# A hybrid stream encoder on one core: sums of squares and turned roots of a recurrence as 64x64 products, with new tables for the order of all its items

## The chip, the cores and the metric

The kernel runs on one NeuronCore of one Trainium2 chip. A core has a matrix engine (TensorE, PE in the profile; its weight loads are shown as an engine of their own, PEld), a vector engine (DVE), a scalar engine (ACT), a GpSimd engine (POOL) and a queue for transfers (SyncE, SP). The metric is the device time of one execution in microseconds (us), as the median of several runs; lower is better.

## The reference

The reference is one inference step of a small encoder in float32: a layer with an RWKV-7 time mixer and a layer with banded attention, each followed by a gated feed-forward part. The change touches the time mixer alone:

```python
kk = heads(k * k_k)
kk = kk / jnp.maximum(jnp.sqrt(jnp.sum(kk * kk, axis=-1, keepdims=True)), 1e-12)
...
def step(S, inp):
    r_t, w_t, k_t, v_t, na_t, b_t = inp
    sa = jnp.einsum('bhvk,bhk->bhv', S, na_t)
    S = S * w_t[:, :, None, :] + sa[..., None] * b_t[:, :, None, :] + v_t[..., None] * k_t[:, :, None, :]
    return S, jnp.einsum('bhvk,bhk->bhv', S, r_t)
...
mean = jnp.mean(out, axis=-1, keepdims=True)
var = jnp.mean(jnp.square(out - mean), axis=-1, keepdims=True)
out = ((out - mean) * lax.rsqrt(var + LNX_EPS)).reshape(B, T, D) * lnx_w + lnx_b
```

There are 16 heads of 64 channels, 1024 prompt frames, and 8 streams of 16 frames: 1152 frames in all. Two sums over the 64 channels of a head are needed for each frame: one of the squared keys (`kk * kk`) and one of the squared, centered outputs (`var`).

## The kernel before

The recurrence (`recurrence_phase`) works on pairs of heads: one pair fills the 128 partitions, head one in partitions 0 to 63 and head two in 64 to 127, with the 1152 frames as columns. There are 8 pairs. The frames are cut into 18 chunks of 64 and, for wide work, into three thirds of 384 columns. Everything is written as a list of items, `(what, pair, argument)`. All engines walk through one list, `ITEMS_ORDER`, in order (TensorE through `TENSOR_ORDER`, the same list with some items joined), and each does its own part of an item; semaphores carry the dependences. So the order of the list is the order of every engine's queue.

The list is made of six threads, each with a letter. A is the serial part (`step`, two parts for each of 16 chunks, and the eight streams' steps `s0t`, `sw`, `so`, `ns`, `nst`). B forms the matrices of a chunk (`form`). C prepares a pair (`w`, `a`, `scan`, `ksum`, `decays`, `kexp`, `k2`, `b`, `write`, `rk`). D finishes a pair (`center`, `vsum`, `affine`, `gate`). E and F invert the chunks' triangular matrices in groups of four chunks, on two lines (`x0`, then `invert` with a half 0 and a half 1 for each level, then `fold`). A string of letters, `PATTERN`, says from which thread the next item comes. It is used for every pair, with the serial part of pair o, the finishing of pair o-1 and most of the forming and inverting of pair o+1. Another string, `FIRST`, comes ahead of it once, and has no A in it.

Three facts of the code matter here.

- `heads` issues two 64x64 products that stay in their head's half (partitions 0 to 63 to 0 to 63, and 64 to 127 likewise). `cross` issues two that change the half. The profile shows a float32 product of these as two matmuls and two weight loads.
- `joined` merges neighbours of the list on TensorE: an `invert` half 1 beside a `form` becomes `both`, a `step` part 0 with an `invert` half 0 right behind it becomes `beside`. In these the products of the two alternate.
- `sums` (L1350) takes the sums of squares as nine 128x128 products with 56 columns of `headones`; `expanded` (L1357) turns the roots of a third back into rows of channels by three 128x128 transposes. `ksum` and `vsum` are one item for a pair each, `kexp` and `affine` three each. Their results go to one PSUM bank, bank 7 (`PIECE_BANKS`), which they share with `w`, `a`, `rk`, `center`, `gate` and others; a piece has to be read before the next is written.

What stands behind a sum: DVE scales the sums (L1779 or L1813) and inverts them (L1781, L1815), ACT takes the root of all 1152 columns (L1697, L1700) after a table load, TensorE turns it (`kexp`, `affine`), DVE multiplies.

Of the kernel before, what the change touches and what calls it, by code (L numbers as in the profile page):

```python
# [373 lines left out]
def front_phase(nc, t, mem, o):  # L374
# [468 lines left out]
SUM_COLS = 56  # L843
# [7 lines left out]
FIRST = (  # L851
    "CCCCCCCCCCCCCCCCCCCCBBBCCCBCCCCBCCEBECBBEBCBCECFFBCFCCFCCFEBFCFCEBCCFCCCBEBEBFCECCFECFECCCE")
PATTERN = (
    "EBADFBAEDABEAFDFEADAFBAEFAAECDADADBFECAFEACFBEBCFAEDAECCAABFAEADAECAFCEADABFCEABECACFAEACEAAEFCAFCAEECABABFAAA"
    "EFACBEACAFBECCAACFACEBBFCAAEAFCEBBECAAEFCEAFEACFCCE")
# [138 lines left out]
def prepare_items(o):  # L994
# [4 lines left out]
    out += [("ksum", o, None)] + [("decays", o, c) for c in range(3)]  # L999
# [4 lines left out]
def finish_items(o):  # L1004
    return [("center", o, c) for c in range(3)] + [("vsum", o, None)] + [("affine", o, c) for c in range(3)] + [("gate", o, c) for c in range(3)]


def last_finish_items():
    o = PAIRS - 1
    center, vsum, rest = (lambda x: (x[:3], x[3], x[4:]))(finish_items(o))  # L1010
    return center + [("ns", o, 1), vsum] + rest[:3] + [("nst", o, 0), ("nst", o, 1)] + rest[3:]
# [18 lines left out]
def recurrence_order():  # L1030
# [30 lines left out]
    for c, after in enumerate((("vsum", o, None), ("affine", o, 2), ("nst", o, 0))):  # L1061
        for_tensor.remove(("gate", o, c))
        for_tensor.insert(for_tensor.index(after) + 1, ("gate", o, c))
# [11 lines left out]
    ("high", 1, "vsum", None), ("high", 5, "vsum", None), ("high", 6, "nst", 0))]  # L1075
PIECE_BANKS = (7, 0, 1, 2, 3, 4)
LAST_BANKS = {("center", 0): 4, ("center", 1): 5, ("ns", 1): 4, ("nst", 0): 5, ("affine", 1): 5, ("affine", 2): 4,
# [4 lines left out]
def recurrence_phase(nc, t, mem, o):  # L1082

    m = recurrence_areas(mem)
    with ExitStack() as ctx:
# [27 lines left out]

        head_sums = lambda pb: pb[:, 0:T // P * SUM_COLS].rearrange("p (i h c) -> p i h c", h=2, c=SUM_COLS // 2)[:, :, :, 0]
        roots = lambda j: m.rs[:, j, :].rearrange("p (i h) -> p i h", h=2)
# [219 lines left out]
        def _(pe):  # L1335
# [53 lines left out]
            def read(pr, n):  # L1389

                pe.wait_ge(outs_done, NCH * pr + n + 1)
                cross(out_of(n), m.s[:, n % 2, :], m.ar[:, pr % 2, n, 64:128], False, False).then_inc(read_done, 1)

# [60 lines left out]
            STREAMED = {("w", 0): 30, ("w", 1): 4, ("w", 2): 4, ("a", 0): 4, ("a", 1): 4, ("a", 2): 4, ("ksum", None): 4,  # L1454
                        ("kexp", 0): 12, ("kexp", 1): 5, ("kexp", 2): 5, ("rk", 0): 28, ("rk", 1): 4, ("rk", 2): 4}
            STREAMED_LAST = {("center", 0): 3, ("ns", 1): 4, ("vsum", None): 4}
            for key in TENSOR_ORDER:
# [6 lines left out]
                if what in PIECES:  # L1464
# [10 lines left out]
                elif what == "ksum":  # L1475
                    pe.wait_ge(kq_ready, pr + 1)
                    sums(pb, m.k2).then_inc(piece_done[b], 1)
                elif what == "kexp":
                    pe.wait_ge(kroot, pr + 1)
# [2349 lines left out]
```

## Time and profile before

| what | us |
|---|---|
| median of 3 runs | 3540.37 (3538.47 to 3543.31) |
| the profiled execution's own time | 3546.33 |
| its span in the profile | 3544.6 |
| TensorE busy (share of the span) | 3381.6 (95%) |
| DVE, ACT, POOL busy | 1652.6, 1354.5, 1740.5 |
| the recurrence in the span | about 412 to 1130 |
| first `step` of pairs 0 to 7 at | 493.9, 570.1, 652.1, 733.1, 812.2, 896.7, 978.6, 1053.9 |

The span is the time from the first to the last instruction. A "busy" engine has at least one instruction under way; matmuls overlap, so a busy TensorE can still go faster. "Idle" is shown with what ended it; "issue" is idle time in which the engine waited for nothing that the profile shows. The granted clock is TensorE's share of its full clock.

### The profile page before, as it was taken

To read this page: it belongs to the slowest core of one execution; us is meant where nothing else is said; L and a number is where in the kernel's file an instruction comes from. 1 tells how busy PE (TensorE), PEld (TensorE's weight loads), DVE (VectorE), ACT (ScalarE), POOL (GpSimd) and SP (SyncE) were. 2 spreads that over 40 slices of the span, in tenths; PEclk is the share of its full clock that TensorE was granted. 3 is DMA by queue.
4 is the path that set the end of the run, shared out by engine and by line. 5 is a ranking of instruction groups with operands and counts; after the bars stand their busy time and mean duration, and the time that the engine had idled before them with its cause. 6 is when DMAs were issued, how large, how long until landed. Compare 5 with 4: busy or idle time off the path is not lost. (4 is left out here: it accounts for less than half of the span.)

```text
span 3544.6 us, 87445 instructions
## 1 busy us (share of the span) xinstructions
PE 3381.6 (95%) x33525; PEld 2940.6 (83%) x33525; DVE 1652.6 (47%) x3032; ACT 1354.5 (38%) x2917; POOL 1740.5 (49%) x1622
## 2 busy tenths in 40 slices
PE   8999889998898999999999999999989999999999
PEld 8999778777777998888888887777769988888887
DVE  7113356555554374444444533333343744444444
ACT  6212445554443133333333434444453333333335
POOL 4434266666654445454554544344433354545455
PEclk9999899999999999999999999999999999999999
DMA  4422211111114011111111234444442111111111
GB/s 154 154 88 89 71 35 36 43 41 38 38 44 143 10 45 46 48 44 45 44 46 47 87 85 96 114 102 91 107 108 66 41 46 47 43 50 42 47 44 73
DMA packets 432743, 233.86 MB, mean 66 GB/s; under 512 B 190979, under 2 KB 417043, under 8 KB 431558
## 3 DMA queue, kind: packets, MB, share of 16 engines
q1 hardware_dynamic: 428882, 215.40, 21.9%
q10 hardware_dynamic: 3572, 14.33, 1.0%
q8 instruction: 215, 3.52, 0.4%
q14 instruction: 74, 0.61, 0.1%
HBM read 187.69 MB, written 47.21 MB: 66 GB/s over the span
## 5 line engine op out<-in xcount | busy, mean ns | idle before, releaser
L2688 DVE TENSOR_TENSOR H<-ps,H 128x512 f32<-128x512 f32 x608 | 419.6, 690 | 463.3 <-PE ps L2351 462.5
L2239 POOL TENSOR_TENSOR split<-work,split 128x512 fp32r<-128x512 f32 x280 | 379.8, 1361 | 493.9 <-ACT split L2510 486.8
L2351 PE MATMUL ps<-split,split 128*128 128x512 f32 x1824 | 514.0, 390 | 0.0
L2404 PE MATMUL ps<-xs,split 128*128 128x512 f32 x1920 | 512.5, 393 | 0.0
L1341 PE MATMUL ps<-arena 64*64 64x64 f32 (+1 forms) x9984 | 400.9, 225 | 37.9 <-issue 21.2
L1341 PEld LDWEIGHTS ps<-arena 64*64 64x64 f32 x9984 | 351.6, 135 | 71.4 <-issue 45.6
L2404 PEld LDWEIGHTS ps<-xs,split 128*128 128x128 f32 x1920 | 349.9, 188 | 68.2
L2351 PEld LDWEIGHTS ps<-split,split 128*128 128x128 f32 x1824 | 339.8, 188 | 70.9 <-DVE H L2688 0.7
L2404 PE MATMUL ps<-split,split 128*128 128x512 f32 x1440 | 366.1, 390 | 0.5 <-issue 0.5
L3278 PE MATMUL ps<-xs,split 128*128 128x384 f32 x1656 | 361.4, 355 | 2.6 <-POOL split L3192 2.6
L601 PE MATMUL ps<-mixed,wsplit_mix 128*128 128x384 f32 x1872 | 331.7, 339 | 7.6 <-DVE mixed L824 7.6
L601 PEld LDWEIGHTS ps<-mixed,wsplit_mix 128*128 128x128 f32 x1872 | 330.1, 189 | 8.9 <-DVE mixed L824 8.9
L1347 PE MATMUL ps<-arena 64*64 64x64 f32 (+3 forms) x4448 | 305.6, 253 | 27.9 <-DVE arena L1853 9.6
L2404 PEld LDWEIGHTS ps<-split,split 128*128 128x128 f32 x1440 | 267.6, 188 | 55.5 <-issue 1.0
L3278 PEld LDWEIGHTS ps<-xs,split 128*128 128x128 f32 x1656 | 277.9, 189 | 30.0 <-issue 22.4
L1347 PEld LDWEIGHTS ps<-arena 64*64 64x64 f32 x4448 | 209.4, 136 | 62.8 <-issue 43.5
L2510 ACT CAST split<-work 128x512 fp32r<-128x512 f32 x280 | 174.0, 622 | 138.8 <-PE ps L2404 107.7
L2244 POOL TENSOR_TENSOR split<-work,split 128x256 fp32r<-128x256 f32 x168 | 132.6, 790 | 173.1 <-ACT split L2517 170.5
L3441 ACT ACTIVATE work<-work,work 128x640 f32<-128x640 f32 (+3 forms) x144 | 101.0, 702 | 257.4 <-DVE work L3532 249.4
L3244 POOL TENSOR_SCALAR work<-work,work 128x640 f32<-128x640 f32 (+2 forms) x64 | 95.0, 1484 | 190.0 <-DVE work L3537 190.0
L95 POOL TENSOR_SCALAR wsplit_mix<-stage_mix 128x1024 fp32r<-128x1024 f32 x26 | 76.1, 2927 | 203.7 <-PE ps L601 171.4
L2548 ACT COPY ps<-ps 128x512 f32<-128x512 f32 x120 | 68.8, 573 | 279.1 <-PE ps L2404 279.1
(325 smaller groups left out, 5972.4 us busy)
## 6 DMA issues: line engine op xcount, KB each, us to landing
work<-in_ffn_w_gu SPq DMA_DIRECT2D x168, 256.0 KB, 2.9
work<-in_ffn_w_down SPq DMA_DIRECT2D x168, 128.0 KB, 2.3
work<-in_cache_v SPq DMA_DIRECT2D x64, 256.0 KB, 3.9
work<-in_cache_k SPq DMA_DIRECT2D x256, 64.0 KB, 2.2
rkv_scratch<-lora ACTq DMA_DIRECT2D x24, 576.0 KB, 2.8
stage_mix<-in_rwkv_w_rkv SPq DMA_DIRECT2D x24, 512.0 KB, 3.8
work<-in_attn_w_qkv SPq DMA_DIRECT2D x24, 512.0 KB, 4.2
h_scratch<-H SPq DMA_DIRECT2D x2, 4608.0 KB, 12.5
```

Source lines behind the costliest of these rows:

```text
L601: last = pe.matmul(mem.ps[:, 4 * v + c, 0:CW], mem.wsplit[:, v, w, k * P:(k + 1) * P], mixed[part][:, k, c * CW:(c + 1) * CW], start=(k == ...
L1341: last = pe.matmul(out[lo:hi], lhsT[lo:hi], rhs[lo:hi] if rhs is not None else eye(lo, hi), start=start, stop=stop)
L1347: last = pe.matmul(out[to:end], lhsT[lo:hi], rhs[lo:hi] if rhs is not None else eye(lo, hi), start=start, stop=stop)
L2239: pool.tensor_tensor(w[1], frm, w[0].bitcast(F32), ALU.subtract).then_inc(u_lo, 1)
L2244: pool.tensor_tensor(w[1], mem.down_raw, w[0].bitcast(F32), ALU.subtract).then_inc(d_lo, 1)
L2351: last = pe.matmul(full(DOWN + j % 2), w[part][:, (m % 2) * P:(m % 2 + 1) * P], mem.hid[xpart][:, SEG[h]], start=(a == 0), stop=(a == 2))
L2404: last = pe.matmul(full(to), unit(i)[part][:, k * P:(k + 1) * P], operand[xpart][:, k, :], start=(first and k == 0 and a == 0), stop=(k == ...
L2510: act.copy(w[0], w[2] if i == 3 else mem.raw[:, RAW_OF[i], :]).then_inc(u_hi, 1)
L2688: dve.tensor_tensor(at, full(DOWN + j % 2), at, ALU.add).then_inc(added, 1)
L3244: pool.tensor_scalar(pr, pr, mem.rinv[:, N % 2, 1:2], None, ALU.mult).then_inc(np_ready, 1)
L3278: last = pe.matmul(ps[:, GEMM + b, 0:CW], mem.wsplit[:, (3 * p + u) % 2, w, k * P:(k + 1) * P], mem.xs[:, part, k, c * CW:(c + 1) * CW], s ...
L3441: act.activation(pr, pr, ACT.Exp, scale=-1.0, bias=mem.mx[:, N % 2, h:h + 1], accum_out=mem.rsum[:, N % 2, h:h + 1]).then_inc(ex_ready, 1)
```

## The change

`ksum` and `vsum` become three items each, one for each third. A third's sum is six `cross` products of a 64-frame block with 16 columns of ones; a third's turn is six `cross` products with the 64x64 identity. DVE scales the sums of each third (128x6) by itself, and inverts all 18 columns after the third one. The table `FIRST` of 91 letters becomes `START` of 248, which holds the whole serial part of pair 0; `PATTERN` is another string, and is used for pairs 1 to 7. The rest of the diff moves code into functions with the same products. The two strings say nothing to a reader; a line of each stands below, and the orders behind it show what they do.

```diff
-FIRST = (
-    "CCCCCCCCCCCCCCCCCCCCBBBCCCBCCCCBCCEBECBBEBCBCECFFBCFCCFCCFEBFCFCEBCCFCCCBEBEBFCECCFECFECCCE")
+START = (
+    "CCCCCCCCCCCCCCCCCCCCCCCCBBBCCBCCBECECBCEBBECEBFCCFCFCECFCFBBECCCEFCCEBFBAEFCCCCEECFBCCFAEAEFACCBEBAFBAAECFACAF"
...
-    out += [("ksum", o, None)] + [("decays", o, c) for c in range(3)]
+    out += [("ksum", o, c) for c in range(3)] + [("decays", o, c) for c in range(3)]
...
-    for letter in FIRST:
+    rest["A"] = serial_items(0)
+    for letter in START:
         out.append(rest[letter].pop(0))
-    for o in range(PAIRS):
-        threads = {"A": serial_items(o) if o + 1 < PAIRS else last_serial_items(), "D": finish_items(o - 1) if o else []}
+    assert not rest.pop("A")
+    for o in range(1, PAIRS):
+        threads = {"A": serial_items(o) if o + 1 < PAIRS else last_serial_items(), "D": finish_items(o - 1)}
...
-            def sums(out, squares):
-
-                for i in range(T // P):
-                    last = pe.matmul(out[:, SUM_COLS * i:SUM_COLS * (i + 1)], squares[:, i * P:(i + 1) * P],
-                                     mem.headones[:, 64 - SUM_COLS // 2:64 + SUM_COLS // 2], start=True, stop=True)
-                return last
-
-            def expanded(out, roots, c):
-
-                for i in range(3):
-                    last = pe.transpose(out[:, i * P:(i + 1) * P], roots[:, (3 * c + i) * P:(3 * c + i + 1) * P], mem.ident[:, :])
-                return last
+            def sums(pb, squares, c, j):
+                return cross(pb[:, TS * j:TS * j + TS], squares[:, c * CW + 64 * j:c * CW + 64 * j + 64], mem.ones[:, 0:TS])
+
+            def expanded(pb, roots, c, j):
+                return cross(pb[:, 64 * j:64 * j + 64], roots[:, c * CW + 64 * j:c * CW + 64 * j + 64], None)
...
+                elif what in ("ksum", "kexp", "vsum", "affine"):
+                    norm_start(what, pr, arg)
+                    for j in range(6):
+                        norm_part(what, pr, arg, j)
...
                 elif what == "ksum":
-                    dve.tensor_scalar(roots(0), head_sums(pb), 1e-24, None, ALU.max).then_inc(piece_free[b], 1)
-                    dve.wait_ge(piece_free[b], n + 1)
-                    dve.reciprocal(m.rs[:, 0, :], m.rs[:, 0, :]).then_inc(kinv, 1)
+                    dve.tensor_scalar(roots(0, arg), head_sums(pb), 1e-24, None, ALU.max).then_inc(piece_free[b], 1)
+                    if arg == 2:
+                        dve.wait_ge(piece_free[b], n + 1)
+                        dve.reciprocal(m.rs[:, 0, :], m.rs[:, 0, :]).then_inc(kinv, 1)
```

On TensorE, the first `vsum` (of pair 0, among the first steps of pair 1) stood so before. L1341 is `heads`, L1347 is `cross`, L1353 the sums; x counts products.

```order
L1341 MATMUL ps<-arena 64x64 x16
L1347 MATMUL ps<-arena 64x64 x6
L1353 MATMUL ps<-headones,arena 128x56 x9
L1347 MATMUL ps<-arena 64x64 x2
L1341 MATMUL ps<-arena 64x64 x8
```

The same place now (L1344 is `heads`, L1350 is `cross`, and the sums are its products with `ones`):

```order
L1350 MATMUL ps<-ones,arena 64x16 x12
L1350 MATMUL ps<-arena 64x64 x2
L1344 MATMUL ps<-arena 64x64 x2
L1350 MATMUL ps<-arena 64x64 x2
L1344 MATMUL ps<-arena 64x64 x2
L1350 MATMUL ps<-arena 64x64 x2
L1344 MATMUL ps<-arena 64x64 x4
L1350 MATMUL ps<-ones,arena 64x16 x12
L1344 MATMUL ps<-arena 64x64 x8
L1350 MATMUL ps<-arena 64x64 x2
L1344 MATMUL ps<-arena 64x64 x6
L1350 MATMUL ps<-ones,arena 64x16 x12
```

One block of nine became three of twelve, with a `step` part 0 and the squares of an `invert` (rows that alternate, now a `beside`), then squares and a step between them.

On TensorE, the turn from pair 0 to pair 1 ended so before: the second `fold` (64x128 x8), the last `form` (the five rows from 64x128 to the identity x4), then `step` (0, 1) with the first squares of groups 2 (L1341 x16), and a `center` (64x384).

```order
L1341 MATMUL ps<-arena 64x128 x8
L1347 MATMUL ps<-arena 64x128 x2
L1347 MATMUL ps<-arena 64x64 x2
L1347 MATMUL ps<-ident,arena 64x64 x2
L1347 MATMUL ps<-arena 64x128 x2
L1347 MATMUL ps<-ident,arena 64x64 x4
L1347 MATMUL ps<-arena 64x64 x2
L1341 MATMUL ps<-arena 64x64 x16
L1347 MATMUL ps<-arena 64x384 x2
```

The same place now, from the first `fold` on:

```order
L1344 MATMUL ps<-arena 64x128 x8
L1350 MATMUL ps<-arena 64x384 x2
L1344 MATMUL ps<-arena 64x128 x8
L1344 MATMUL ps<-arena 64x64 x2
L1350 MATMUL ps<-arena 64x64 x2
L1350 MATMUL ps<-arena 64x384 x2
L1350 MATMUL ps<-arena 64x64 x2
L1344 MATMUL ps<-arena 64x64 x8
```

The forms of chunks 16 and 17 have left this place; they stand a few steps later, joined to two halves of an `invert`. Fewer products stand between the first `fold` and the squares of group 2.

## Rows read from the trace of the kernel before

**Rows 1.** The page: its first line.

```profile
span 3544.6 us, 87445 instructions
```

**Rows 2.** Windows, TensorE: stretch, length, busy time, matmuls, granted clock, DMA share, GB/s.

```profile
412.00:493.90 81.90, 67.80 (x1094) 0.85 0.24 75
...
570.10:652.10 82.00, 74.09 (x2195) 1.00 0.15 41
...
978.60:1053.90 75.30, 67.66 (x2148) 1.00 0.08 21
```

**Rows 3.** TensorE's waits from 541 to 1040: for whom, us, times, longest.

```profile
PE ps L1341 <- issue: 17.3, 21, 1.5
PE ps L1347 <- DVE arena L1853: 7.0, 6, 1.8
PE ps L1347 <- issue: 5.6, 8, 1.8
PE ps L1341 <- DVE arena L1843: 4.2, 12, 0.6
PE ps L1341 <- POOL arena L1320: 3.9, 9, 0.6
```

**Rows 4.** Timeline of TensorE around a sum: start, length, instruction, matmuls.

```profile
741.45 0.39 PE L1347 MATMUL ps<-arena 64*64 64x64 f32 x7
741.77 2.21 PE L1353 MATMUL ps<-headones,arena 128*128 128x56 f32 x18
743.92 0.27 PE L1347 MATMUL ps<-arena 64*64 64x64 f32 x2
```

**Rows 5.** The same around a turn of a third.

```profile
748.85 0.55 PE L1360 MATMUL ps<-ident,arena 128*128 128x128 f32 x3
749.33 0.27 PE L1347 MATMUL ps<-arena 64*64 64x64 f32 x2
```

**Rows 6.** Windows of single items: squares with a step, `both`, `form`, sixteen matmuls of `nst`.

```profile
755.36:755.84 0.48, 0.48 (x30) 1.00 0.00 0
757.46:758.41 0.95, 0.95 (x71) 1.00 0.08 17
...
694.11:694.84 0.73, 0.73 (x31) 1.00 1.08 372
729.59:730.05 0.46, 0.46 (x23) 1.00 0.00 0
```

**Rows 7.** Timeline: `cross` products with 16 columns in a row.

```profile
715.01 0.47 PE L1347 MATMUL ps<-arena 64*64 64x16 f32 x10
```

**Rows 8.** From 541 to 1040: transfers of instructions, and TensorE's matmuls.

```profile
q8 instruction: 110, 1.80, 1.5%
```

```profile
541.00:1040.00 499.00, 451.50 (x13597) 1.00 0.13 37
```

**Rows 9.** Timeline: two idle times by "issue"; then windows between such ends.

```profile
626.56 0.62 PE L1341 MATMUL ps<-ident,arena 64*64 64x64 f32 x14 [1.42 <-issue]
630.71 0.50 PE L1347 MATMUL ps<-arena 64*64 64x64 f32 x10 [1.02 <-issue]
```

```profile
626.56:630.71 4.15, 3.13 (x125) 1.00 0.19 51
...
638.52:642.44 3.92, 3.18 (x125) 1.00 0.02 4
```

**Rows 10.** POOL's groups from 541 to 1040 that start a group of chunks.

```profile
L1311 POOL TENSOR_TENSOR arena<-arena 128x256 f32<-128x256 f32 x50 | 37.1, 742 | 54.5 <-PE ps L1341 52.5
L1312 POOL TENSOR_TENSOR arena<-arena 128x512 f32<-128x512 f32 x25 | 31.7, 1268 | 2.0
```

**Rows 11.** Timeline of DVE behind the sum of rows 4.

```profile
744.03 0.18 DVE L1813 TENSOR_SCALAR arena<-ps 128x18 f32<-128x18 f32 x1 [2.03 <-PE ps L1353]
```

**Rows 12.** Timeline of TensorE in the first pair: its longest waits for data.

```profile
492.65 0.76 PE L1341 MATMUL ps<-arena 64*64 64x128 f32 x10 [1.80 <-DVE arena L1843]
497.64 0.27 PE L1347 MATMUL ps<-arena 64*64 64x64 f32 x2 [2.02 <-DVE arena L1853]
```

More of the change, by code:

```diff
@@ L1060, in recurrence_order @@
     for_tensor = list(out)
[L1061 removed]
+    for c, after in enumerate((("vsum", o, 2), ("affine", o, 2), ("nst", o, 0))):
         for_tensor.remove(("gate", o, c))
@@ L1392, in read, with fold_start, fold_part @@
                 cross(out_of(n), m.s[:, n % 2, :], m.ar[:, pr % 2, n, 64:128], False, False).then_inc(read_done, 1)
+            def fold_start(pr, g):
+                pe.wait_ge(tm_ready, chunks_after(pr, g))
+                pe.wait_ge(x_ready[LINE[g]], xs_before(pr, g) + LEVELS[g] + 1)
+            def fold_part(g, q):
+                c0, line = GROUPS[g][0], LINE[g]
+                return heads(bank[:, M[line], q * 128:(q + 1) * 128], m.xy[:, line, q, 0:64], m.slots[:, c0 + q, 256:384])
             def step_start(pr, n):
@@ L1463, in _ @@
                 e = pr % 2
-                if what in PIECES:
+                if what in PIECES and what not in ("ksum", "kexp", "vsum", "affine"):
                     b, n = PIECE_OF[key]
@@ L1474, in _ @@
                     last.then_inc(piece_done[b], 1)
[L1475 to L1479, printed above, removed]
-                    expanded(pb, m.kkn, arg).then_inc(piece_done[b], 1)
+                elif what in ("ksum", "kexp", "vsum", "affine"):
+                    norm_start(what, pr, arg)
+                    for j in range(6):
+                        norm_part(what, pr, arg, j)
                 elif what == "rk":
@@ L1490, in _ @@
                     cross(pb[:, 0:CW], m.center, third(m.out, arg)).then_inc(piece_done[b], 1)
-                elif what == "vsum":
-                    for c in range(3) if pr == PAIRS - 1 else (2,):
-                        cb, cn = PIECE_OF["center", pr, c]
-                        pe.wait_ge(piece_free[cb], cn + 1)
-                    sums(pb, m.post1).then_inc(piece_done[b], 1)
-                elif what == "affine":
-                    pe.wait_ge(vroot, pr + 1)
-                    expanded(pb, m.post1, arg).then_inc(piece_done[b], 1)
                 elif what == "gate":
@@ L1554, in _ @@
                 elif what == "fold":
-                    g = arg
-                    (c0, G), line = GROUPS[g], LINE[g]
-                    pe.wait_ge(tm_ready, chunks_after(pr, g))
-                    pe.wait_ge(x_ready[line], xs_before(pr, g) + LEVELS[g] + 1)
-                    for q in range(G):
-                        last = heads(bank[:, M[line], q * 128:(q + 1) * 128], m.xy[:, line, q, 0:64], m.slots[:, c0 + q, 256:384])
-                    last.then_inc(folded[line], 1)
+                    fold_start(pr, arg)
+                    for q in range(GROUPS[arg][1]):
+                        last = fold_part(arg, q)
+                    last.then_inc(folded[LINE[arg]], 1)
                 elif what == "step":
@@ L1691, in _ @@
                     act.copy(m.vb[:, e, c0:c0 + G, :], part(m.v)).then_inc(written_act, 1)
-                elif what == "ksum":
+                elif what == "ksum" and arg == 2:
                     if pr:
@@ L1697, in _ @@
                     act.activation(blocks(m.kkn), m.rs[:, 0, :].unsqueeze(2).to_broadcast((P, 18, 64)), ACT.Sqrt).then_inc(kroot, 1)
-                elif what == "vsum":
+                elif what == "vsum" and arg == 2:
                     act.wait_ge(vinv, pr + 1)
@@ L1812, in _ @@
                 elif what == "vsum":
-                    dve.tensor_scalar(roots(1), head_sums(pb), 1.0 / HD, LNX_EPS, ALU.mult, ALU.add).then_inc(piece_free[b], 1)
-                    dve.wait_ge(piece_free[b], n + 1)
-                    dve.reciprocal(m.rs[:, 1, :], m.rs[:, 1, :]).then_inc(vinv, 1)
+                    dve.tensor_scalar(roots(1, arg), head_sums(pb), 1.0 / HD, LNX_EPS, ALU.mult, ALU.add).then_inc(piece_free[b], 1)
+                    if arg == 2:
+                        for c in range(3):
+                            vb, vn = PIECE_OF["vsum", pr, c]
+                            dve.wait_ge(piece_free[vb], vn + 1)
+                        dve.reciprocal(m.rs[:, 1, :], m.rs[:, 1, :]).then_inc(vinv, 1)
                 elif what == "affine":
```

47 lines of the change are left out of this document (35 added, 12 removed).

## The prediction

> **What bounds the kernel now.** I read the page first, then windows by pair, then TensorE's waits. The span is 3544.6 us [rows 1]; the recurrence takes about 412 to 1130 of it, and nothing else changes. Cut at the first `step` of each pair, six periods lie between 570.1 and 1053.9, the first and the last of them in [rows 2]: 483.8 us, so 80.6 us each. TensorE is busy 74.1 of 82.0 us at full clock: it bounds the recurrence, and what a period costs is TensorE's own work plus its waits. Of waits there are two kinds [rows 3]. For data: 7.0 us behind L1853 (DVE's copy for a `step`), 4.2 behind L1843, 3.9 behind POOL's L1320, some 20 us with the small ones over 499 us, or 3.2 a period. And "issue": 17.3 + 5.6 us, with a small rest 23.5, or 3.8 a period.
>
> What "issue" is can be read off. Queue q8 carries 110 transfers of instructions, 1.80 MB, so 16 KB each, while TensorE runs 13597 matmuls and as many weight loads [rows 8]: 27194 / 110 is 247 a transfer, and with the waits about 256, so 64 bytes an instruction. Between the ends of two such idle times lie 125 matmuls and as many loads [rows 9], again one transfer's worth. So TensorE runs blocks of 256 instructions, and waits when it finishes one before the next has come. Blocks with such a wait took 3.9 to 4.7 us, those of [rows 9] 4.15 and 3.92; the work in them, without the wait, took 3.13 and 3.2. I put the least time of a block at about 3.9 us.
>
> **The products.** A sum of squares now: the last cross product ahead of it starts at about 741.6, the first one behind it at 743.92, with the sum from 741.77 [rows 4]. From the start of the sum to the next product are 2.15 us, and about 0.15 us to get into it: 2.3 us. A 64x64 product pair in a row costs by [rows 6] 0.46 us for 16 matmuls, 29 ns a matmul; with 16 columns 10 matmuls take 0.47 us with the last one's own 0.21, again 29 ns [rows 7]. So fewer columns save nothing. A third is 12 products, 24 matmuls: 0.70 us, a whole sum 2.1. A turn took 748.85 to 749.33 [rows 5], 0.48 us, and 0.15 to get in: 0.63; it becomes 0.70. Per period: sums 2 x (2.1 - 2.3) = -0.4, turns 6 x 0.07 = +0.4. Bounds: `heads` and `cross` use different quarters of the array and overlap at a border, as 16 matmuls of squares and 12 of a `step` did, 28 in 0.48 us [rows 6], 17 ns each. If each of the 12 new runs gained 0.15 us at its borders, that would be -1.8; if none did, 0. I take -0.6.
>
> **The order.** Counted in the list of a period: `both` 13 to 15, `beside` 2 to 10. A whole `both` takes 0.95 us against 0.73 for the `form` alone [rows 6] and 32 x 0.029 = 0.93 for the updates. But both orders have 12 whole ones; the two more are short (16 updates: 0.73 + 0.47 - 0.95), 0.25 us each: -0.5. A `beside` joins what overlaps at its border anyway (0.48 us for 28, above). Against no overlap (28 x 0.029 = 0.81) it could save 0.3 each, or 2.4; against the row, nothing. I take -0.1 each: -0.8. TensorE's work: -1.9 a period, between -0.5 and -4.7.
>
> **The instructions.** This speaks against the change. Before, sums and turns of a period were 36 + 18 matmul records; now they are 144 + 144. That is 234 more matmuls and 234 more loads, 468 / 256 = 1.8 more blocks on 17.8 (110 blocks over 6.2 periods). A block's own time, waits for instructions left out, was (80.6 - 3.8) / 17.8 = 4.3 us on the mean and becomes (76.8 - 1.9) / 19.6 = 3.8 us, just under the 3.9 that a block needs. The old sums and turns, few instructions in much time, were where transfers caught up. Going through the 108 blocks between 541 and 1040, the shortfalls under 3.9 us add up to 23 us, as the rows show; with every block's time cut to 0.885 of itself, and a tenth more blocks, they add up to 40 to 46: +2.7 to +3.7 a period. Some of it takes the place of waits for data. I take +2.2; bounds: 0 (if dense and thin stretches alternate luckily) and +3.7.
>
> The Trainium skill (Runtime: NRT & Kernel Launch, section Instruction fetch mechanics) says that instructions come in 16 KiB blocks of 256, which the rows bear out, and that crossing a boundary is "mostly hidden", which they don't. By the page this term would be 0; what the whole comes to without it stands under B below.
>
> **Waits for data.** Leaving the turn from pair to pair, `form` 16 and 17 no longer stand ahead of DVE's copy for `step` (0, 1); of the 7.0 us behind L1853 [rows 3], 1.1 a period, I count -0.7. DVE stood 2.03 us before a sum [rows 11], with a `step`'s work behind it; now at most a third of that at a time: -0.3. Against this, the squares of group 2 need POOL's work behind the first `fold`: two L1311 of 0.74, one L1312 of 1.27 and one more like the first, 3.5 us and the hand-overs [rows 10]. Between them stood two items of about 0.8 us more than now: +0.8; at worst +1.5, if POOL also comes late to the second line's squares behind it. DVE gets four short operations of 0.18 us more a period [rows 11], POOL and ACT nothing; DVE is not late. Bank 7 has 34 pieces a period, not 30; between two thirds of `ksum` stand only 0.3 to 1 us of work, perhaps +0.2. Sum: 0 a period, from -2.5 to +2.
>
> **First and last pair.** From 412 to 493.9 TensorE is busy 67.8 of 81.9 us at 0.85 of the clock [rows 2], and the worst waits are 1.80 us for the last inverse and 2.02 for the first `step` [rows 12]. `START` puts steps of pair 0 among the last inverses, and turns of pair 1: I count -5 for waits, -2 for more joined items, +1.5 for instructions. But the first three sums and turns have nothing to hide behind: three thirds through one bank, each with DVE's 0.18 us and two hand-overs, +2.5. Together -3, from -9 to +5. At the end, the last pair's sum can start a third at a time; -1.
>
> **The sum.** Six periods of -1.9 + 2.2 + 0 = +0.3 are +2; -3; -1: -2 to -3 us. The profiled execution took 3546.33 and would take about 3544; it stood 6 us above the median, so the median goes from 3540.4 to about **3538**.
>
> **The rivals.**
> *A, about even,* as summed: 0.38, its own range 3528 to 3548.
> *B, the order wins.* The two strings together hold TensorE's whole order; if they remove 2 us of waits for data a period (of 3.2 there are) and the border gains come in, a period loses 3 us more: -15 to -25. The same time comes if instructions do not get in the way: 6 x -2.2 and -1.5 in the first pair on the sum give -15. So 3523, with 3513 as the far end. For it: the old waits are few but concentrated at the turn and in the first pair. Against: the fetch rows. 0.31.
> *C, instructions win; slower.* If the blocks cost their full +3.7 a period, and POOL's wait at the turn of the pair its +1.5, a period is 80.6 - 1.9 + 3.7 + 1.5 - 0.3, or +3.0: +18 and -4, 3554. It decides from the point where the mean block's own time falls under 3.9 us, which the sum reaches. For it: 21 + 8 idle times of this kind already [rows 3], each behind a dense stretch. 0.31.
> That the products change nothing in TensorE's time but add a tenth to its instructions is part of A and C.
>
> **How the numbers follow.** A measurement here tells about 0.2%, 7 us, from no change. Faster: all of B and 0.07 of A's 0.38: 0.38. Slower: C and 0.02 of A: 0.33. Within: 0.29. The range takes in most of B and C: 3512 to 3562.
>
> **What the profile would show.** No L1353 or L1360 group; `cross` products with 16 columns, 24 matmuls in about 0.70 us; about 121 blocks where there were 110 in as many periods, and more "issue": 35 us or so for 23.5 in six periods if A holds, 45 for C, 25 for B. The periods, first `step` to first `step`: 80 to 81 us for A, 77 to 78 for B, 83 to 84 for C. Pair 0's first `step` early, and pair 1's at 565 to 568 rather than 570.1. At the turn of a pair, TensorE waits over 1 us for L1320's successor, and hardly for L1853's. I am wrong if the "issue" time stays, or if waits for data change by over 2 us a period.

## The result, and the profile after

The changed kernel takes 3590.99 us (median of 4 runs, 3588.12 to 3593.32); the kernel before took 3539.63 in the same comparison. The ratio is 1.0143, 95% interval 1.0125 to 1.016: slower by 51 us, where 3538 was predicted, and outside the range. The two profiled executions took 3592.12 and 3546.33 us, 46 us apart: that of the kernel before stood 7 us above its median. What follows from the traces has to be added up to 46, not to 51.

Its first page line, the answer to [rows 1]:

```profile
span 3590.3 us, 91277 instructions
```

The first steps of pairs 0 to 7 are now at 483.0, 576.9, 663.2, 752.7, 839.3, 927.6, 1016.0 and 1096.6 us. The first comes 10.9 us sooner than before, pair 1's is 6.8 us late, six periods follow of 86.6 us instead of 80.6 (36 us in all), and behind the last first step stand 77.0 us instead of 72.4.

TensorE's waits from 541 to 1085, 6.28 periods (answers to [rows 3]; who waits, for whom, us, times, longest):

```profile
PE ps L1344 <- issue: 27.0, 32, 1.7
PE ps L1350 <- DVE arena L1875: 17.2, 12, 3.1
PE ps L1350 <- issue: 9.9, 15, 1.3
PE ps L1350 <- ACT arena L1723: 6.2, 6, 1.2
PE ps L1344 <- DVE arena L1865: 4.9, 12, 1.0
PE ps L1344 <- POOL arena L1323: 4.4, 9, 0.6
```

"Issue" is 36.9 us, 5.9 a period where it was 3.8. Waits for data, with the small ones, are 37.8 us or 6.0 a period where they were 3.2. These windows do not end with a period; over the six periods exactly, "issue" is 24.4 us before (4.1 a period) and 34.3 after (5.7), and the waits for data are 3.1 and 5.9 a period. Two rows are new: the copy L1875 for a `step` (7.0 us before as L1853, in the same number of turns), and L1723, ACT's reading of a `center` from bank 7.

Both stand at the turn between pairs. TensorE there (start, length, instruction, and in brackets the idle time ahead and what ended it):

```profile
751.10 0.76 PE L1344 MATMUL ps<-arena 64*64 64x128 f32 x10 [1.04 <-DVE arena L1865]
...
754.33 0.86 PE L1350 MATMUL ps<-arena 64*64 64x384 f32 x4 [1.15 <-ACT arena L1723]
758.29 0.30 PE L1350 MATMUL ps<-arena 64*64 64x64 f32 x2 [3.10 <-DVE arena L1875]
```

In the kernel before, the same two waits of TensorE were these, for the copy and for POOL's operand of the next squares:

```profile
735.53 0.27 PE L1347 MATMUL ps<-arena 64*64 64x64 f32 x2 [0.34 <-DVE arena L1853]
...
736.78 0.51 PE L1341 MATMUL ps<-arena 64*64 64x64 f32 x10 [0.56 <-POOL arena L1320]
```

DVE behind the last inverse, now:

```profile
751.21 0.69 DVE L1818 SCALAR_TENSOR_TENSOR arena<-arena 128x252 f32<-128x252 f32 x1
751.82 0.67 DVE L1823 TENSOR_TENSOR arena<-arena 128x256 f32<-128x256 f32 x1
752.41 0.94 DVE L1818 SCALAR_TENSOR_TENSOR arena<-arena 128x252 f32<-128x252 f32 x1
753.28 0.94 DVE L1823 TENSOR_TENSOR arena<-arena 128x256 f32<-128x256 f32 x1
754.14 1.48 DVE L1818 SCALAR_TENSOR_TENSOR arena<-arena 128x252 f32<-128x252 f32 x1
755.54 0.94 DVE L1823 TENSOR_TENSOR arena<-arena 128x256 f32<-128x256 f32 x1
756.41 0.86 DVE L1821 SCALAR_TENSOR_TENSOR arena<-arena 128x60 f32<-128x60 f32 x2
757.20 0.81 DVE L1823 TENSOR_TENSOR arena<-arena 128x128 f32<-128x128 f32 x1
757.94 0.21 DVE L1875 COPY arena<-ps 128x64 f32<-128x64 f32 x1
```

The `step` (0, 0) was issued at 752.69. Its copy, 0.21 us long, stands behind `write` 1 to 4 of the next pair, and starts 5 us later. In the old order these writes also came ahead of the copy, but with halves of an `invert` between them, and with a `fold` and a `form` between the last of them and the `step`; now only a `center` and a `fold` stand there.

Then the windows (columns as in [rows 2]), from the turn on and for the six periods:

```profile
750.00:751.00 1.00, 0.06 (x3) 0.00 (x0) 1.00 (x3) 0.81 (x4) 1.00 (x2) 1.00 0.31 66
...
757.00:758.00 1.00, 0.00 (x0) 0.00 (x0) 1.00 (x4) 0.00 (x0) 0.84 (x3) 1.00 0.87 332
758.00:759.00 1.00, 0.71 (x18) 0.74 (x20) 0.41 (x3) 0.00 (x0) 1.00 (x1) 0.71 0.64 232
759.00:760.00 1.00, 1.00 (x32) 0.90 (x32) 0.19 (x2) 0.35 (x1) 1.00 (x3) 0.50 0.00 0
...
762.00:763.00 1.00, 1.00 (x37) 0.93 (x34) 0.47 (x2) 0.64 (x3) 1.00 (x1) 1.00 0.00 0
```

```profile
660.00:680.00 20.00, 14.06 (x457) 12.75 (x452) 12.23 (x27) 10.75 (x29) 15.44 (x17) 0.91 0.24 63
740.00:780.00 40.00, 32.20 (x1026) 28.25 (x1030) 26.79 (x54) 15.59 (x45) 29.88 (x34) 0.96 0.13 33
840.00:860.00 20.00, 15.38 (x502) 14.38 (x504) 11.15 (x26) 9.05 (x22) 12.61 (x13) 0.83 0.17 50
920.00:940.00 20.00, 15.27 (x420) 13.85 (x414) 14.37 (x27) 9.06 (x29) 18.98 (x22) 0.83 0.23 62
1020.00:1040.00 20.00, 16.45 (x608) 15.63 (x612) 9.84 (x27) 7.20 (x16) 10.44 (x11) 0.91 0.03 6
```

This is what the prediction has no word for. After the idle stretch of the turn, the granted clock falls to 0.50, the lower of its two levels (1.2 GHz), while TensorE is fully busy again. The five windows add up to 20 x 0.09 + 40 x 0.04 + 20 x 0.17 + 20 x 0.17 + 20 x 0.09 = 12 us of full-speed time not granted, 2.0 a period. That is an upper estimate of the loss, since TensorE was not busy in all of it. The same stretch of the kernel before has 1.00 in all of them:

```profile
570.10:1053.80 483.70, 436.71 (x13093) 375.29 (x13091) 273.40 (x642) 233.51 (x616) 293.89 (x356) 1.00 0.14 38
```

These are single executions, but the mean clock of all runs tells the same: 0.985 in the four of the changed kernel, 0.988 to 0.989 in 19 of the kernel before. Of 3591 and 3542 us, 54 and 41 were not granted, 13 more.

TensorE's busy time over the six periods is 436.7 us before and 444.1 after:

```profile
576.90:1096.60 519.70, 444.14 (x14384) 387.01 (x14382) 289.81 (x657) 232.57 (x614) 294.96 (x354) 0.98 0.13 36
```

So the 6.0 us of a period are: waits for data +2.8, issue +1.6, idle times too short to be listed +0.4, busy time +1.2. Up to 2.0 of the busy time is the clock, which leaves about -0.8 for TensorE's own work at full clock.

### The profile page after: what moved, and what is told of

It is laid out like the page before. It is cut to its first block and busy times, and to the rows that moved or that the text cites. A ratio compares the mean times of both kernels' runs of the same rounds, so it can differ in the third digit from the quotient of the medians.

```text
span 3590.3 us, 91277 instructions
## 1 busy us (share of the span) xinstructions
PE 3386.6 (94%) x35397; PEld 2950.2 (82%) x35397; DVE 1673.8 (47%) x3064; ACT 1354.3 (38%) x2917; POOL 1742.3 (49%) x1622
## 5 line engine op out<-in xcount | busy, mean ns | idle before, releaser
L1344 PE MATMUL ps<-arena 64*64 64x64 f32 (+1 forms) x9984 | 421.7, 230 | 49.7 <-issue 26.7
L1344 PEld LDWEIGHTS ps<-arena 64*64 64x64 f32 x9984 | 368.6, 138 | 79.9 <-issue 51.4
L1350 PE MATMUL ps<-arena 64*64 64x64 f32 (+2 forms) x4448 | 317.2, 256 | 47.2 <-DVE arena L1875 19.1
L1350 PEld LDWEIGHTS ps<-arena 64*64 64x64 f32 x4448 | 213.3, 137 | 81.4 <-issue 47.8
```

Of the source, the lines that this page charges most:

```text
L1344: last = pe.matmul(out[lo:hi], lhsT[lo:hi], rhs[lo:hi] if rhs is not None else eye(lo, hi), start=start, stop=stop)
L1350: last = pe.matmul(out[to:end], lhsT[lo:hi], rhs[lo:hi] if rhs is not None else eye(lo, hi), start=start, stop=stop)
```

## The experiments

All times are medians, and "over before" is against the kernel before, measured beside each.

| kernel | us | over before | ratio, 95% interval |
|---|---|---|---|
| e1_products | 3567.84 | +26.8 | 1.0046 to 1.0097 |
| e2_order | 3565.74 | +24.7 | 1.0046 to 1.0095 |
| e3_old_start | 3591.87 | +50.8 | 1.0119 to 1.0167 |
| e4_turn | 3585.54 | +44.5 | 1.0105 to 1.0159 |
| e5_sums_only | 3545.66 | +7.2 | 1.0006 to 1.0034 |
| e6_turns_only | 3551.82 | +13.4 | 1.0023 to 1.0050 |
| e7_turn2 | 3587.03 | +48.6 | 1.0107 to 1.0156 |
| e8_no_beside | 3590.54 | +52.1 | 1.0115 to 1.0163 |
| e9_k2_early_turn2 | 3589.25 | +47.5 | 1.0106 to 1.0167 |
| e10_k2_early | 3592.93 | +51.2 | 1.0121 to 1.0181 |
| e11_pad128 | 3614.98 | +73.2 | 1.0176 to 1.0235 |
| e12_old_products | 3569.30 | +27.5 | 1.0052 to 1.0098 |
| e13_forms_back | 3576.98 | +35.8 | 1.0069 to 1.0143 |
| e14_before_pad128 | 3530.40 | -10.8 | 0.9961 to 0.9990 |
| e15_before_pad64 | 3529.93 | -11.2 | 0.9948 to 0.9978 |
| e16_after_pad128 | 3589.57 | +48.4 | 1.0109 to 1.0163 |
| e17_before_forms_away | 3549.90 | +7.2 | 1.0015 to 1.0042 |
| e18_forms_back_k2 | 3585.29 | +42.6 | 1.0106 to 1.0146 |

### Products or order

The old order with the new products (one letter of each set becomes three):

```diff
-START = (248 letters), PATTERN = new
+START = FIRST and the old PATTERN without D, PATTERN = old, with three C for ksum and three D for vsum
```

> The new products in the old order: ksum and vsum are three items, each third as 64x64 products, with the two extra items of each set one to three places ahead of the old one. Theory: the order made the new waits for data (+2.9 us a period, and the first and last pair), the products the added issue time (+2.2 a period). Then this kernel is 10 to 20 us over the one before: six periods of about +2.3, and 0 to +5 outside them, with the copy L1875 costing TensorE no more than the 7 us of before over 541 to 1040. Rival (the products carry the loss, through bank 7's pieces and denser code): 35 to 50 us over, and issue time over 8 us a period or new waits for DVE and ACT.

The new order with the old products:

```diff
-    for letter in FIRST:
+    rest["A"] = serial_items(0)
+    for letter in START:
```

> The new order with the old products: one ksum and one vsum for a pair, at the place of the last of the three; START and PATTERN otherwise as in the changed kernel. Theory: this carries the waits for data, so it is 25 to 35 us over the kernel before, with the issue time near the old 3.8 us a period and the copy for step (0,0) waited for by about 3 us at each turn. Rival (products carry the loss): within 7 us of the kernel before, or faster.

The changed kernel with the old first pair (e1's START with the new PATTERN):

> The changed kernel with the old order for the first pair (the old FIRST and PATTERN written out, with three ksum items), new PATTERN for pairs 1 to 7. If START costs what stands before pair 1's first step (576.9 against 570.1), this is 5 to 8 us faster than the changed kernel, so 43 to 46 over the kernel before; if START itself is neutral and the products cost there, it is within 3 us of the changed kernel; if START is good by itself (first step at 483 and not 494), it is 3 to 10 us slower.

26.8 and 24.7 add up to the whole 51; the intervals leave each some 9 us either way. Neither side of my theory's split holds for the products, which cost more than its 10 to 20, and START by itself is neutral. The order's part is what was read at the turn: in e2 the copy costs 17.0 us with the longest 3.1, ACT's reading 6.2, as in the changed kernel; the issue time is less than before, 2.6 a period.

```profile
PE ps L1351 <- DVE arena L1857: 17.0, 12, 3.1
PE ps L1345 <- DVE arena L1847: 9.4, 25, 0.7
PE ps L1345 <- issue: 9.0, 10, 1.6
```

Its clock falls too: five windows of 20 us in its six periods have 0.83, 0.91, 0.91, 0.91 and 0.83, again 12 us.

### Sums or turns

One kind of new product at a time, in the old order. In both, one side changes the half and the other doesn't, so the two heads' scales are exchanged: part of the computation is changed, the amount of work is not.

```diff
             def expanded(pb, roots, c, j):
-                return cross(pb[:, 64 * j:64 * j + 64], roots[:, c * CW + 64 * j:c * CW + 64 * j + 64], None)
+                return pe.transpose(pb[:, j * P:(j + 1) * P], roots[:, (3 * c + j) * P:(3 * c + j + 1) * P], mem.ident[:, :])
```

> The old order with the new sums alone (three items, 64x64 products with 16 columns); the turns are the three 128x128 transposes of before. Products alone cost 27 us together. Theory: what costs is time and blocks of the turns, which were 0.48 us and are 0.53 to 0.9 for a third, with 252 more instructions a period; the sums are even (1.98 for 2.15 us) and only add 216 instructions and two more pieces in bank 7. So 5 to 12 us over the kernel before. Rival (the sums' smaller pieces wait for bank 7 and for DVE, and carry the loss): 18 us or more over.

```diff
-                for i in range(3):
-                    last = pe.transpose(out[:, i * P:(i + 1) * P], roots[:, (3 * c + i) * P:(3 * c + i + 1) * P], mem.ident[:, :])
+                for j in range(6):
+                    last = cross(out[:, 64 * j:64 * j + 64], roots[:, c * CW + 64 * j:c * CW + 64 * j + 64], None)
```

> The kernel before with the new turns alone: kexp and affine as six 64x64 cross products for each third, sums as nine 128x56 products. Theory: the turns carry the larger share, 14 to 20 us over the kernel before: 6 x 0.25 us a period of TensorE's work, +1 of issue. Rival: under 7 us over, and the sums carry the loss.

+7.2 and +13.4, and 6 more when both are there. The first is inside its expected range and the second just under its own; the turns carry more, as expected. For the turns alone (541 to 1065, 6.31 periods of 83.1 us):

```profile
PE ps L1341 <- issue: 17.9, 24, 1.4
PE ps L1347 <- issue: 13.3, 15, 2.6
PE ps L1347 <- DVE arena L1853: 7.6, 5, 2.0
PE ps L1347 <- DVE arena L1818: 4.8, 12, 0.4
```

Issue went from 3.8 to 4.9 a period, and the second and third turn of a set wait twice as long for DVE to read bank 7 (L1818, 2.5 us before). With the new sums alone it went the other way, to 15.2 us over 541 to 1040 or 2.5 a period, though they too add 216 instructions. So the issue time doesn't follow the number of instructions alone. In the profiled executions the clock takes its part: it is 0.66 from 820 to 835 in e5 and 0.74 from 660 to 680 in e6, 5 us each, and 9 us are missing in four windows of e1. Over all ten runs the mean clock is 0.987 for e5 and 0.989 for e6, where the kernel before has 0.989: of e6's 13 us the clock holds nothing in the mean, of e5's 7 us most.

### The turn between pairs

Three ways to take the wait for the copy away (e4, e7, e9), and `k2` early by itself (e10). Three writes later:

```diff
-    "DEFADAAEFDAEDAFDEADACBF..."  ...CEFCACECC
+    "DEFADAAEFDACEDAFDCEADACCBF..."  ...CEFCAE
```

> The changed kernel with three items moved: write 2, 3 and 4 of a pair leave the end of PATTERN and follow step (1,1), vsum 1 and step (3,0) of the next turn. So DVE's copy for step (0,0) no longer stands behind six of the writes' operations. Theory (the writes make the copy late): the 17 us behind that copy in 541 to 1085 fall to 5 or less, and the kernel is 10 to 14 us faster than the changed one, some 38 over the one before. Rival (the writes only move, and DVE's copies for steps (2,0) to (4,0) are late in their place): within 4 us of the changed kernel.

The turn written anew, without and with `k2` early (and `k2` early alone):

```diff
-    "DEFADAAEFDA..."  ...CEFCACECC
+    "EADFCCDAEAFDA..."  ...CEFCACE
```

```diff
-    out += [("ksum", o, c) for c in range(3)] + [("decays", o, c) for c in range(3)]
-    out += [("kexp", o, c) for c in range(3)] + [("k2", o, None), ("b", o, None)] + ...
+    out += [("ksum", o, c) for c in range(3)] + [("k2", o, None)] + [("decays", o, c) for c in range(3)]
+    out += [("kexp", o, c) for c in range(3)] + [("b", o, None)] + ...
```

> The changed kernel with the turn between two pairs written anew: x0 of group 2 and step (0,0) stand right behind the first fold and ahead of write 3 and 4, then a center, the second fold, write 3 and 4, a center, step (0,1), squares of group 2, step (1,0). POOL gets x0 earlier and its writes no later than now plus that; DVE makes its copy for step (0,0) ahead of the last two writes. Theory: both waits of the turn go, 17 us for the copy and most of the 6 us for ACT's reading of bank 7, and POOL's waits stay near 5: 12 to 20 us faster than the changed kernel. Rival (POOL and DVE have no room at a turn; a wait only moves, as it moved to POOL's operands of the inverses when three writes were put behind the steps): within 5 us of the changed kernel, with POOL's L1323 or DVE's updates over 15 us.

> The changed kernel with the turn of e7_turn2 and k2 moved ahead of decays (behind the last ksum and s0t 0, some 35 items earlier). In the changed kernel POOL is idle for 7.7 us at 724.5 to 732.3 and then runs without a gap through k2 (1.30 + 2.64 us), b, ten operations of the writes and x0 up to the squares of group 2; with the kernel before, k2 began at 713.5 and POOL still had 1.6 us free at the turn. Theory (POOL's pile ahead of the turn is what the turn waits for, and DVE's copy only hid it): the 25 us behind POOL's L1323 fall to 8 or less and no wait takes their place: 3563 to 3575 us, 15 to 25 faster than the changed kernel. Rival (something else is late next, an inverse's DVE operation or ACT): within 8 us of the changed kernel.

> k2 moved ahead of decays alone, the turn as in the changed kernel. Theory: the copy for step (0,0) still stands behind the writes on DVE, but the writes of DVE and POOL no longer overlap with a late pile, so a part goes: 5 to 12 us faster than the changed kernel, with the copy still waited for by 1.5 to 3 us at a turn. Rival (POOL's pile is not the bound): same as the changed kernel within 4 us.

The copy's 17 us are gone in e4, e7 and e9 (1.6 in each), and the time hardly moves: 22.1, 25.4 and 25.9 us are now waited for POOL's L1323, the operand of the next squares. `k2` early brought nothing. POOL's timeline in e9 says why:

```profile
747.44 0.72 POOL L1280 TENSOR_TENSOR arena<-arena 128x256 f32<-128x256 f32 x1
751.60 1.58 POOL L1314 TENSOR_TENSOR arena<-arena 128x256 f32<-128x256 f32 x2 [3.43 <-PE ps L1344]
753.26 1.33 POOL L1315 TENSOR_TENSOR arena<-arena 128x512 f32<-128x512 f32 x1
```

POOL was done early and idle for 3.43 us: `x0` overwrites what the `fold` on its line reads, so it can't start before that fold ends, at 751.6. Fold, `x0` (2.9 us), operand (0.7 us), squares is a chain, and in the kernel before two `form` (0.73 us for one in [rows 6]) stood over it, those of chunks 16 and 17. The change took them away.

Both forms back at the turn:

```diff
-    "DEFADAAEFDA..."
+    "EABDFBDAECAFDAC..."   (two B less behind it, two C less at the end)
```

> The changed kernel with the turn written anew and the forms of chunks 16 and 17 back in it: fold, x0, step (0,0), form 16, center, fold, form 17, center, step (0,1), squares of group 2, write 3, step (1,0), x0, center, step (1,1), write 4. Theory: the chain fold, x0 on POOL (2.9 us), POOL's operand (0.7 us), squares needs 3.7 us of other work on TensorE, and the two forms (0.85 us each) are what the new order took from it: POOL's 25 us fall under 12 with nothing in their place, 3565 to 3578 us (13 to 25 faster than the changed kernel). Rival (the forms' own DVE operations delay the copy, or POOL's later operands come late): within 8 us of the changed kernel.

14 us were won of the 51, more than by any other repair. The four runs spread from 3570.87 to 3589.29, and the six periods of the profiled one are 8 us shorter (85.2 us each). Against e7, which has nearly the same turn without the two forms, it is 10 us, and the last two writes stand elsewhere too; so the forms' own share is not known better than that. 16.6 us are left behind POOL, which has `write` 3 right ahead of the second `x0` and `write` 4 right behind it. With these put back ahead of the first `x0`, and `k2` early:

> The changed kernel with the two forms back at the turn, k2 ahead of decays, x0 ahead of step (0,0), and the writes in their place. POOL's pile ahead of the turn is 3.9 us shorter, so it should be done with write 4 when the first fold is (about 751), and nothing stands between x0, the operands and the squares. Theory: POOL's waits under 8 us and the copy's under 8, 3562 to 3574 us, so that nearly the whole 25 us of the order are undone. Rival (one of the two stays late, as in the other repairs): 3575 or more.

```profile
PE ps L1350 <- ACT arena L1723: 26.3, 6, 5.2
...
PE ps L1344 <- POOL arena L1323: 4.5, 7, 1.0
PE ps L1350 <- DVE arena L1875: 1.5, 7, 0.2
```

POOL and the copy are free now, and ACT is late with the `center`: its part of form 16 waited 5.14 us for DVE's (L1858), which stood behind the same writes. Read so, the writes' ten DVE operations are the load of the turn, and what is queued behind them decides who shows the wait; no run took that load away, so this was not tested.

The counter-test, the two forms taken away from the turn of the kernel before:

> The kernel before with the forms of chunks 16 and 17 moved from the turn (behind x0 and behind the second fold) to a place behind step (1,0) and behind step (2,0), and the three forms behind them one place later each; nothing else. Theory (these forms cover the chain from the fold over POOL's x0 and its operand to the squares of group 2): POOL's L1320 costs over 10 us in 541 to 1040 where it cost 3.9, and the kernel is 8 to 18 us slower than before. Rival (the old order has room at the turn): within 5 us of the kernel before.

```profile
PE ps L1347 <- DVE arena L1853: 12.2, 6, 2.3
...
PE ps L1341 <- POOL arena L1320: 4.3, 6, 1.8
```

It is 7.2 us slower, short of the 8 to 18 of the theory. And the wait went elsewhere than said: 12.2 us are waited for the copy where there were 7.0, and behind POOL's L1320 there are 4.3 us, not over 10. In the profiled execution the six periods are 2.4 us longer each (83.0), 14 us in all, but up to 9 of these are the clock (five windows of 20 us at 0.91 where there were none). Over its ten runs the mean clock is 0.987, that of the kernel before 0.988, so the clock has little part in the 7 us of the medians.

The new order of e9 with the old products (e12) is a last look at the split: 3569.3, no better than e2, with 29.0 us now waited for POOL.

> The order of e9_k2_early_turn2 with the old products (one ksum, one vsum, 128x56 sums, transposes). The old products were worth 25 us in the changed order (3565.7 for 3591). If the two repairs add up: 3540 to 3550, no slower than the kernel before. If the turn costs in both but the fetch of instructions takes back what the waits gave: 3555 or more.

### The joined items

```diff
-        elif before and before[0] == "step" and before[2][1] == 0 and before[2][0] and key[0] == "invert" and key[2][2] == 0:
-            out[-1] = ("beside", before[1], (before, key))
```

> The changed kernel without the joining of a step's part 0 with the squares behind it (no beside; the order of the items is the same, both stays). The prediction counted -0.1 us for each of eight more besides in a period. The windows so far have the work of beside, step, invert, both and form at 50.0 us a period in the new order and 48.7 in the old one, so joining seems to bring nothing. Theory: within 4 us of the changed kernel. Rival (a beside does save): 5 to 15 us slower than the changed kernel; or (it costs, since a step's products are held up behind squares) 5 us faster or more.

Within 1 us of the changed kernel: ten `beside` a period are worth nothing that these runs can tell. I had counted -0.8 a period for eight of them, 5 us in six.

### The blocks of instructions

```diff
+            for _ in range(128):
+                pe.wait_ge(consts, 16)
```

> The changed kernel with 128 waits on a semaphore that has long been reached, put ahead of the recurrence's first TensorE instruction: half a block of 256 instructions, nothing else. If issue waits are the coming of blocks of instructions, they stand at other products than before, half a block off, and their sum over six periods may change by several us either way, since the same shortfalls meet other neighbours; the whole time within 8 us. Rival (the issue waits belong to the products they stand before, such as a change of the array's quarters): the waits stay before the same items, and so does their sum, within 1 us a period.

```diff
+            for _ in range(64):   # 32 in e15
+                pe.matmul(bank[:, OB, 0:16], plain_ones[:, 0:P], plain_ones[:, 0:16], start=True, stop=True)
```

> The kernel before with 64 small bf16 products (16 columns; 64 matmuls and 64 weight loads, so 128 instructions) ahead of its recurrence, where TensorE waits for weights anyway. Theory (the offset of the blocks matters): period and issue change by 0.5 to 2.5 us a period against 80.6 and 4.1, likely upwards if the kernel before has been picked by its time: 3545 to 3557 us. Rival (the offset does not matter here, and what e11 lost was the waits themselves): within 4 us of the kernel before.

> The same with 32 small products, a shift of 64 instructions. Same theory: another period again, 3540 to 3555 us; the spread over the three offsets (0, 64, 128) is the share of the difference that is luck. Rival: within 4 us of the kernel before.

> The changed kernel, shifted by 128 instructions with 64 small products in place of waits. Theory: the small products are hidden, so the 16 us that e11 lost ahead of pair 1's first step shrink to 3 or less, while the periods are 88.4 us as in e11: 8 to 14 us slower than the changed kernel. Rival (e11's periods came from something else than the offset): within 4 us of the changed kernel.

e11's 128 waits were not free, and they were not half a block: the trace has 64 instructions more (91341 for 91277). They fill a stretch of 23.66 us where otherwise there are 2.32, 0.17 us for each:

```profile
430.99 5.09 PE L1482 MATMUL ps<-ones 128*128 128x256 bf16 x30 [23.66 <-issue]
```

What "issue" is can be settled by counting. Number TensorE's instructions as they stand in the trace, matmuls, loads and waits: in every kernel here, each of the 18 to 50 waits (0.15 us or more) by "issue" between 541 and 1085 us stands at instruction 165 to 169 of a block of 256. e16 has 48 of them and the changed kernel 47, and not one stands at the same product; most are 61 to 63 matmuls off, which is the half block of the shift. So they belong to the blocks, and the rival (the products' quarters of the array) is out.

With products in place of the waits (e16) the offset alone is seen: the periods of the changed kernel go from 86.6 to 87.6 us, issue in the six of them from 34.3 to 40.7 us (38.5 in e11), the whole time not at all. In the kernel before, the periods go from 80.6 to 80.0 (e14) and 80.5 (e15), where longer ones were expected, and issue in six from 24.4 to 15.6 and 18.3 us. So an offset moves the issue time by 4 to 9 us in six periods and the period by up to 1 us (1.8 in e11, 88.4), and the kernel before was not a lucky one. Over the three offsets of each, issue is 16 to 24 us before and 34 to 41 after.

e14 and e15 are 11 us faster than the kernel before, against the expectation, and as fast as each other. Of this, 7.7 us lie ahead of the first step (486.2 in e14 for 493.9): the granted clock there is 0.94 and 0.83 where it was 0.73 and 0.67.

```profile
412.00:430.00 18.00, 16.24 (x108) 9.46 (x106) 3.10 (x5) 7.99 (x11) 1.52 (x2) 0.94 0.57 186
430.00:450.00 20.00, 13.99 (x179) 11.49 (x178) 12.93 (x21) 6.71 (x23) 16.50 (x16) 0.83 0.10 34
```

e17, whose code up to there is that of before, has 1.00 and 0.83 in these windows, and its first step at 483.7, so this clock also changes from one execution to the next. Before and after were both profiled with the low one, 0.73 and 0.74, and can be compared.

## Why the prediction was wrong

**The step that failed first is "Waits for data: 0 a period, from -2.5 to +2".** It came out at +2.8. Within it, "form 16 and 17 no longer stand ahead of DVE's copy, I count -0.7" had the wrong sign: with these forms moved away and nothing else (e17), the wait for the copy went from 7.0 to 12.2 us, +0.9 a period. The two forms were cover for the turn. "DVE is not late" looked at how many operations DVE gets, not at where the `write` items moved: close in front of the copy, 5 us of DVE's time. The +0.8 for POOL's `x0` was the right chain, too small, and hidden at first behind the copy; e7 and e9 show it at about 4 us a turn. The 1.0 us for bank 7 at a `center` was not counted for the turn at all.

**The clock was no term.** Up to 12 us in six periods, a third of what these lost. It mostly follows the waits: before, no stretch between the first steps of pairs 1 and 7 was below 1.00; after, there is one behind most turns, where TensorE was busy for only 3 of 8 us (750 to 758). In e1 it falls also where it waited less: behind one issue wait of 1.31 us at 642.97 or 1.37 at 814.45, and behind several close together (1.78 for the copy, 0.75 for ACT, 1.23 of issue from 749.78 to 756.70). So a wait of 3 us at a turn costs up to 6, an estimate: 3.1 us of waiting, and 3 more not granted where the clock is at 0.50 from 844 to 850. The Trainium skill (TensorE: Matmul & The Clock Gate, the part on the HAM clock gate) says that the default state is throttled and that activity releases the throttle; the rows agree. That it is the idle time that lets the clock fall was not tested by itself, and the kernel before does not always keep its clock: e14 and e15, its own order with a few small products ahead, have two and four windows of 20 us at 0.91 in their six periods, 4 and 7 us.

**Instructions: +2.2, measured +1.6.** The count of blocks was right, the size only in part by its reason. In one execution each, the products with the old order added 0.4 a period, the new sums alone took 1.6 off, the turns added 0.9, the order alone took 1.5 off, and both together added 1.6. But an offset of 64 or 128 instructions alone moves it by up to 1.5, so none of these differences can be put down to its edit. What stands is that three offsets give 16 to 24 us before and 34 to 41 after, some 3 a period, within the prediction's bounds of 0 to +3.7. Blocks of 256 instructions are what the rows show (121 transfers of instructions in the 544 us, and every such wait at one place of a block); the sum depends on which dense stretches meet which block, and can't be had from a count. The Trainium skill's "mostly hidden" (Runtime: NRT & Kernel Launch, section Instruction fetch mechanics) is not borne out: 5.7 us of each 86.6.

**TensorE's work: -1.9 (bounds -0.5 to -4.7).** At full clock it comes to about -0.8, inside the bounds. What was wrong in it: `beside` is worth 0, not -0.8 (e8). The new pieces had their predicted price, 24 matmuls in 0.67 us for a third of a sum, and 0.65 to 0.75 us for the turn of a third.

**First and last pair: -4, measured +11.** Pair 0's first step did come 10.9 us sooner, but this was given back before pair 1's, and e3 says that START changed nothing in sum. The last pair's 4.6 us come with the products (75.8 us behind the last first step in e1, 72.1 in e2).

**The rivals.** C (slower, 3554) had the right sign and two of the right places, and would have been 14 us over before; it was priced from waits without the clock. "I am wrong if waits for data change by over 2 us a period" is what came.

Between 3538 and 3591 lie 53 us. The six periods hold 34 of them (+36 for the +2 counted) and the two ends 15; the rest is no more than one execution differs from the next. Of the 34, waits for data are 17 and the clock up to 12.

The products' 27 us are only half settled: 7 for the sums, 13 for the turns, and the 6 that come when both are there were not taken apart further. Nor did any repair bring back more than 14 of the order's 25 us, so the mechanism of the rest is read from the rows and stays open.

## What to carry to other kernels

When one order drives the queues of all engines, look for what stood over a chain before you move it away, and list, for each engine, what now stands ahead of the short operation that the bound engine waits for; a wait that one engine gives up goes to the next one unless the load itself is moved. Price a wait of the matrix engine with the slow clock that may follow it. Split a change with two ideas in it (products, order) first of all: two kernels told here that each cost half.

## What the runs showed of the hardware

- 128 semaphore waits of TensorE that had long been fulfilled took 21.3 us in a row, 0.17 us each; the trace has them as 64 instructions.
- TensorE's idle times by "issue" stand 256 instructions apart, or a multiple of it, whatever the products there are (positions 165 to 169 of a block in all twenty kernels, between 541 and 1085 us).
- The clock is behind much of what one execution differs from the next: of 19 runs of the kernel before, the one with a mean clock of 0.985 took 3555.91 us, the eight with 0.990 or more 3531.92 to 3540.26.
- The same 128x256 operation of DVE took 0.41 us alone and mostly 0.94 us while POOL was busy with its own in the same arena (L1823: 0.41 us at 748.70 in e9, 0.94 us at 753.28 after), so the writes cost DVE about double where both engines do them together. The Trainium skill (GPSIMD Engine Reference, section Key points) has it that GpSimd shares its SBUF interfaces with DVE; the factor of two for these operations is from the rows.
- In the first 38 us of the recurrence the granted clock differs from one execution to the next: 0.73 and 0.67 (412 to 430 and 430 to 450) in the kernel before, 1.00 and 0.83 in e17, whose code is the same up to there and whose first step came 10 us sooner. e14 and e15, with small products ahead, had 0.91 to 0.94 and 0.83 and were 11 us faster over ten runs each, at a mean clock of 0.990 to 0.991 for 0.988 to 0.989; e16, with the same products ahead of the changed kernel, had 0.90 and 0.67 and was no faster. That the products brought the higher clock is not shown.
